# Late modulation rows summed on GpSimd from the channel stage on, and the scores of four memory steps kept for the other direction

## What is computed

```python
mod = silu(c) @ w_ada + b_ada                       # 6 * 1024 numbers: sh1, sc1, g1, sh2, sc2, g2
u = layernorm(x) * (1 + sc1) + sh1
proj = u @ w_in                                     # q, k, v, o, gates and the latents of attention
q, k = silu(conv5(proj[q, k]) + conv_b)             # along the tokens, a channel at a time
h = mlstm_scan(q, k, v, i_fw, f_fw) + flip(mlstm_scan(flip(q, k, v), i_bw, f_bw))
# one step of a scan, on a chunk of 128 tokens:
#   w   = exp(d_log - m_t)                          (128 x 128, masked to the past)
#   s   = (q k^T) * w
#   num = a * (q C) + s v ;  h = num / max(|den|, exp(-m_t))
#   C  <- decay * C + (k * wg)^T v
x = layernorm(alpha * x + (1 + g1) * mixer(u));  u = layernorm(x) * (1 + sc2) + sh2   # then the experts, with g2
```

## Time and profile before

| | us |
|---|---|
| median of 3 runs | 1534.51 (1533.08 to 1534.63) |
| the profiled execution | 1535.46, its span 1533.5 |
| TensorE busy | 1487.1 (97% of the span) |
| VectorE busy | 565.2 (37%) |
| ScalarE busy | 357.5 (23%) |
| GpSimd busy | 97.5 (6%) |

### The profile page before, as it was taken

The page is one execution under the profiler, slowest core; times in us unless marked ns, Lnnn a source line. Parts: engine busy times, 40 slices in busy tenths (PEclk is TensorE's granted clock), DMA queues, the critical chain, the costliest instruction groups (busy, mean ns, idle before and its releaser), DMA issues. The chain is left out here.

```text
span 1533.5 us, 19984 instructions
## 1 busy us (share of the span) xinstructions
PE 1487.1 (97%) x7403; PEld 818.7 (53%) x7404; DVE 565.2 (37%) x1134; ACT 357.5 (23%) x738; POOL 97.5 (6%) x97
## 2 busy tenths in 40 slices
PE   7999999999989999999999899999999999999997
PEld 4555554447868666674555554444444444444443
DVE  2222126567769433334867711111011011011118
ACT  1122122137624344352111010110111111111111
POOL 0000002000000000000000011111111111111110
PEclk9999999999999999999999899999999999999999
DMA  9401011128730200004111589869789879999965
GB/s 343 159 28 41 0 8 31 41 69 248 248 114 2 110 0 0 0 0 154 76 56 55 192 344 391 370 243 415 317 327 425 314 314 414 423 385 399 425 282 208
DMA packets 101798, 305.51 MB, mean 199 GB/s; under 512 B 18353, under 2 KB 61661, under 8 KB 92536
## 3 DMA queue, kind: packets, MB, share of 16 engines
q1 hardware_dynamic: 93064, 287.08, 48.6%
q0 software_dynamic: 8064, 16.80, 3.0%
q10 hardware_dynamic: 624, 1.03, 0.2%
HBM read 289.86 MB, written 25.76 MB: 206 GB/s over the span
## 5 line engine op out<-in xcount | busy, mean ns | idle before, releaser
L1908 PE MATMUL ps<-w_down_sb,hidT 128*128 x320 | 153.4, 612 | 0.0
L457 PE MATMUL ps<-w_in_tok,uT 128*128 128x512 f32 (+2 forms) x384 | 141.5, 529 | 0.0
L1892 PE MATMUL ps<-w_gate_sb,x_slotsT 128*128 x320 | 140.7, 593 | 0.7 <-ACT x_slotsT L1991 0.7
L1892 PE MATMUL ps<-w_up_sb,x_slotsT 128*128 x320 | 140.6, 592 | 0.0
L1563 PE MATMUL ps<-uT,hT 128*128 128x512 f32 x256 | 112.8, 594 | 0.0
L624 PE MATMUL ps<-uT,mod 128*128 128x512 f32 x256 | 111.0, 594 | 0.8 <-PEq L213 0.8
L2145 DVE TENSOR_TENSOR hid<-silu_g,ps 128x512 f32<-128x512 f32 x20 | 13.8, 688 | 258.0 <-PE ps L1892 258.0
L457 PEld LDWEIGHTS ps<-w_in_tok,uT 128*128 128x128 f32 x384 | 72.7, 190 | 65.3 <-issue 43.9
L1892 PEld LDWEIGHTS ps<-w_gate_sb,x_slotsT 128*128 128x128 f32 x320 | 60.8, 190 | 76.8 <-issue 76.8
L1892 PEld LDWEIGHTS ps<-w_up_sb,x_slotsT 128*128 128x128 f32 x320 | 60.9, 190 | 76.5 <-issue 76.5
L1908 PEld LDWEIGHTS ps<-w_down_sb,hidT 128*128 128x128 f32 x320 | 55.9, 189 | 65.1 <-issue 64.3
(11 more groups left out here) (405 smaller groups left out, 1926.7 us busy)
## 6 DMA issues: line engine op xcount, KB each, us to landing
light_gate_sb<-in_w_gate SPq DMA_DIRECT2D x20, 2048.0 KB
light_up_sb<-in_w_up SPq DMA_DIRECT2D x20, 2048.0 KB
light_down_sb<-in_w_down SPq DMA_DIRECT2D x20, 2048.0 KB
w_gate_sb<-in_w_gate SPq DMA_DIRECT2D x12, 2048.0 KB
w_up_sb<-in_w_up SPq DMA_DIRECT2D x12, 2048.0 KB
w_down_sb<-in_w_down SPq DMA_DIRECT2D x12, 2048.0 KB, 23.1
mod<-in_w_ada SPq DMA_DIRECT2D x8, 1024.0 KB, 8.1
w_ada_late<-in_w_ada SPq DMA_DIRECT2D x8, 1024.0 KB, 6.8
```

The lines of the kernel that those rows point to most:

```text
L457: mm = nc.tensor.matmul(ps[:, 2 + g, 0:n], self.uT[:, k, t * P:(t + 1) * P], wt[:, k, c0:c0 + n], start=k == 0, stop=k == KD - 1)
L1892: m = m_.matmul(ps[:, bank, :], xT[:, k, :], wt[:, bass.ds(buf, 1), k, :].rearrange("p a f -> p (a f)"), start=k == 0, stop=k == KD - 1)
L1908: m = m_.matmul(ps[:, 5 + half, :], hT[:, k, :], wd[:, bass.ds(buf, 1), k, half * 512:half * 512 + 512].rearrange("p a f -> p (a f)"), sta ...
```

## The change

- The sum over the eight slices of a piece moves from TensorE to GpSimd (`late_part`): it multiplies the tile by `ca` (spread over the 256 columns) in place, then adds 4 + 4, 2 + 2 and 1 + 1 slices. It leaves one row to a partition in `late_parts` (8 places). `spread` then sums over the partitions with a matrix of ones. `partial` and ScalarE's copy go.
- Pieces 0 to 7 are summed in the channel stage, pieces 8 to 15 in the memory stage, where piece n waits for `spread(n - 8)`. SP issues the loads of pieces 0 to 8 between the channel weights; those from piece 2 on wait until the tile that they overwrite has been summed. `LATE_HOME` says which of the two tiles a piece has; in the channel stage the second is `qkT[:, 6:8]`, so the silu of chunk 6 waits for piece 5.
- `scores` runs for steps 0 to 3 only. ScalarE copies each to `hdir` (`kept`), in the place of the other direction's rows of that chunk, and `weighted` of steps 4 to 7 reads it there.

```diff
...
+AHEAD = 8
+LATE_HOME = (0, 1, 0, 1, 0, 1, 0, 0, 0, 1, 0, 1, 0, 1, 0, 1)
...
+        self.w_late0 = pieces(self.mod[:, 0:2, :])
+        self.late_parts = self.sb("late_parts", [P, AHEAD, PC], ctx=up)
+        w_late = [self.w_late0, pieces(self.qkT[:, 6:8, :])]
...
+                def modulation(n, free):
+                    if free:
+                        sp.wait_ge(self.s_lpart, free)
+                    at = EARLY * 512 + n * PC
+                    sp.dma_start(w_late[LATE_HOME[n]], w_ada[:, :, at:at + PC]).then_inc(self.s_lw[LATE_HOME[n]], 16)
+                modulation(0, 0)
                 weights(2)
+                modulation(1, 0)
                 weights(3)
+                modulation(2, 1)
+                modulation(3, 2)
                 sp.wait_ge(s_atc, 2)
...
                 weights(4)
+                modulation(4, 3)
                 weights(5)
+                modulation(5, 4)
                 sp.wait_ge(s_M, 2)
...
                 weights(6)
+                modulation(6, 5)
                 weights(7)
+                modulation(7, 7)
...
-                sp.dma_start(self.w_late0, w_ada[:, :, EARLY * 512:EARLY * 512 + PC]).then_inc(self.s_lw[0], 16)
+                modulation(8, 8)
...
             @block.gpsimd
             def _(pool):
...
                 nc.gpsimd.tensor_tensor(self.hm[:], self.hm[:], mg.unsqueeze(1).to_broadcast([P, TT, H * HD]), ALU.mult).then_inc(s_gm, 1)
                 pool.wait_ge(s_gm, 1)
+                ch = Chain(pool, s_lsum)
+                for n in range(AHEAD):
+                    self.late_part(pool, ch, n, w_late[LATE_HOME[n]])
+                    pool.wait_ge(self.s_lpart, n + 1)
...
             @block.tensor
             def _(pe):
...
                     act.wait_ge(s_cv[j], c // 2 + 1)
+                    if c == 6:
+                        act.wait_ge(self.s_lpart, 6)
                     a.activation(self.qkT[:, c, :], acc[:, j, :], ACT.Silu).then_inc(s_act[j], 1)
...
+    def late_part(self, pool, ch, n, w):
+        g = self.nc.gpsimd
+        pool.wait_ge(self.s_lw[LATE_HOME[n]], 16 * LATE_HOME[:n + 1].count(LATE_HOME[n]))
+        ch.link(g.tensor_tensor(w, w, self.ca[:].unsqueeze(2).to_broadcast([P, KD, PC]), ALU.mult))
+        ch.link(g.tensor_tensor(w[:, 0:4, :], w[:, 0:4, :], w[:, 4:8, :], ALU.add))
+        ch.link(g.tensor_tensor(w[:, 0:2, :], w[:, 0:2, :], w[:, 2:4, :], ALU.add))
+        g.tensor_tensor(self.late_parts[:, n % AHEAD, :], w[:, 0, :], w[:, 1, :], ALU.add).then_inc(self.s_lpart, 1)
     def mlstm(self, up):
...
-            part = sb("late_partial", [P, PC])
...
             @block.sync
             def _(sp):
                 def modulation(n):
-                    if n > 1:
-                        sp.wait_ge(s_lp, n - 1)
+                    if n > AHEAD + 1:
+                        sp.wait_ge(s_lpart, n - 1)
...
-                    sp.dma_start(w_late[n % 2], w_ada[:, :, at:at + PC]).then_inc(s_lw[n % 2], 16)
+                    sp.dma_start(w_late[LATE_HOME[n]], w_ada[:, :, at:at + PC]).then_inc(s_lw[LATE_HOME[n]], 16)
...
                 def maxima(i, d):
...
                 maxima(*HALVES[2])
                 maxima(*HALVES[3])
                 bias(0)
-                modulation(1)
+                modulation(AHEAD + 1)
                 maxima(*HALVES[4])
                 maxima(*HALVES[5])
                 for k in range(len(HALVES) - 2):
-                    modulation(k + 2)
...
                         maxima(*HALVES[k + 6])
+                    if k % 2 == 0 and 2 <= k <= 12:
+                        modulation(AHEAD + 1 + k // 2)
...
                         bias(k // 4 + 1)
...
-                sp.wait_ge(s_lp, len(HALVES) - 1)
+                sp.wait_ge(s_lpart, len(HALVES) - 1)
...
+            @block.gpsimd
+            def _(pool):
+                ch = Chain(pool, s_lsum)
+                for n in range(AHEAD, len(HALVES)):
+                    pool.wait_ge(s_ls, n - AHEAD + 1)
+                    self.late_part(pool, ch, n, w_late[LATE_HOME[n]])
...
             @block.scalar
             def _(act):
...
+                def kept(i, d):
+                    if i >= TT // 2:
+                        return
+                    act.wait_ge(S["p"][d], i + 1)
+                    a.copy(self.hdir[:, 1 - d, chunk(i, d), :], ps[:, d, :]).then_inc(s_keep[d], 1)
...
+                kept(0, 0)
                 for k in range(len(HALVES)):
...
                         decays(*HALVES[k + 3])
-                    act.wait_ge(s_lp, k + 1)
-                    if k > 0:
-                        act.wait_ge(s_ls, k)
-                    a.copy(part[:], ps[:, 7, 0:PC]).then_inc(s_lpc, 1)
...
                         keys(*HALVES[k + 2])
+                    if k + 1 < len(HALVES):
+                        kept(*HALVES[k + 1])
...
             @block.tensor
             def _(pe):
...
                 def scores(i, d):
+                    if i >= TT // 2:
+                        return
                     if i > 0:
...
+                        pe.wait_ge(s_keep[d], i)
...
-                def partial(n):
-                    pe.wait_ge(s_lw[n % 2], 16 * (n // 2 + 1))
+                def spread(n):
+                    pe.wait_ge(s_lpart, n + 1)
...
-                    for k in range(KD):
-                        j = 32 * (k % 4)
-                        m = t.matmul(ps[j:j + 32, 7, 0:PC], self.ca[:, k:k + 1].to_broadcast([P, 32]), w_late[n % 2][:, k, :], start=k < 4, stop=k >= 4)
-                    m.then_inc(s_lp, 1)
-                def spread(n):
-                    pe.wait_ge(s_lpc, n + 1)
-                    t.matmul(ps[:, 7, PC:2 * PC], self.c(C_SUM), part[:], start=True, stop=True).then_inc(s_ls, 1)
+                    t.matmul(ps[:, 7, PC:2 * PC], self.c(C_ONE), self.late_parts[:, n % AHEAD, :], start=True, stop=True).then_inc(s_ls, 1)
...
                 scores(0, 0)
                 key_turns(0, 0)
                 scores(0, 1)
-                partial(0)
                 key_turns(0, 1)
...
                     outer(i, d)
-                    if k > 0:
-                        partial(k)
                     memory(i, d)
...
                         scores(*HALVES[k + 2])
...
                 def weighted(i, d):
-                    dve.wait_ge(S["sc"][d], i + 1)
+                    if i < TT // 2:
+                        dve.wait_ge(S["sc"][d], i + 1)
+                        kq = ps[:, d, :]
+                    else:
+                        dve.wait_ge(s_keep[1 - d], TT - i)
+                        kq = self.hdir[:, d, chunk(i, d), :]
...
                     if i > 0:
...
-                    v.scalar_tensor_tensor(out=p[:, d], in0=ps[:, d, :].rearrange("p (h t) -> p h t", h=H), scalar=QSCALE, in1=w[:, d],
+                    v.scalar_tensor_tensor(out=p[:, d], in0=kq.rearrange("p (h t) -> p h t", h=H), scalar=QSCALE, in1=w[:, d],
...
```

More of the change, by code:

```diff
@@ L528, in project_channels @@
         self.s_lw = [self.sem(f"w_ada_late_loaded{j}") for j in range(2)]
-        self.w_late0 = self.mod[:, 0:2, :].rearrange("p a (k n) -> p (a k) n", n=PC)
+        self.s_lpart = self.sem("late_part_summed")
+        s_lsum = self.sem("late_channel_sums")
+        pieces = lambda ap: ap.rearrange("p a (k n) -> p (a k) n", n=PC)
+        self.w_late0 = pieces(self.mod[:, 0:2, :])
+        self.late_parts = self.sb("late_parts", [P, AHEAD, PC], ctx=up)
+        w_late = [self.w_late0, pieces(self.qkT[:, 6:8, :])]
         w_ada = self.i["w_ada"].rearrange("(p k) n -> p k n", k=KD)
@@ L822, in mlstm @@
         s_v, s_c0 = self.sem("ml_dve"), self.sem("ml_state0")
+        s_keep = [self.sem(f"ml_scores_kept{d}") for d in range(2)]
         s_lw = self.s_lw
         s_lb = [self.sem(f"b_ada_late_loaded{r}") for r in range(4)]
-        s_lp, s_lpc, s_ls, s_late = (self.sem(n) for n in ("late_partial", "late_partial_copied", "late_spread", "late_ready"))
+        s_lsum, s_ls, s_late = (self.sem(n) for n in ("late_sums", "late_spread", "late_ready"))
+        s_lpart = self.s_lpart
         w_ada = self.i["w_ada"].rearrange("(p k) n -> p k n", k=KD)
```

## The result

The changed kernel takes **1579.37 us** (median of 4 runs, 1577.6 to 1582.11) against 1534.57 us (4 runs, 1533.08 to 1535.36): a ratio of 1.0295 with an interval of 1.0281 to 1.0309, slower. 1586 was forecast, in a range of 1521 to 1606. The profiled execution took 1577.74 us with a span of 1575.9 us, 42.4 us more than before.

A forecast was written before the change was run, and what follows sets the result against it. TensorE was taken as the bound, VectorE close behind. Span 1533.5 + 33 (channel stage) + 18 (memory stage) = 1584.5; with 1.96 outside the span 1586.5, so 1586 us against the median, range 1521 to 1606.

The forecast's parts named there:

- The hold: Both stages: VectorE operations with both inputs in SBUF wait until the running GpSimd operation ends, as L723 did.
- Rival one: Both stages: two-input operations are not held; +4 and -17.9, 1521 us, if no tap exceeds 1.4 us; chance 0.21.
- Rival two: Both stages: VectorE gets the exclusive port repeatedly, `a_by_head` nearly on time, GpSimd late; +24 and +5, 1564 us; chance 0.13.
- 29 us for `a_by_head`: Channel stage, before the third chunk: VectorE and GpSimd alternate, so TensorE resumes at 280.5 instead of 251.37.
- +2 for the clock: Channel stage: after 29 us idle TensorE's granted clock falls, costing 2 us.
- +2 for piece 7: Channel stage's end: piece 7 runs against the last convolution, exposing up to a 4.4 us operation; 2 us taken.
- 33: Channel stage in total: 29 + 2 + 2 us later, bounds +4 and +40.
- +18 for the memory stage: Memory stage: net 18 us longer with pieces 8 to 15 on GpSimd; bounds -17.9 and +32.
- 17.9: Memory stage without contention: 72.2 us against 90.1, so 17.9 us saved.
- beside other work: Memory stage, ScalarE: 16 copies go and 8 of 128x512 (0.59 us for one that size) come, beside other work.
- the path followed: Memory stage: half and piece in step at 9.7 us, eight pieces 78 us, seven halves left; 112 us, +22.
- the random case: Memory stage with waits at random instead: a half 7.8 us, ten done by 82.6, five left; +13.

The follow-up runs named there:

- the writes: Changed kernel with GpSimd's operations on each piece replaced by memsets of about the same time; no total compared, marks at 345.66 and 425.99, memory stage 80.3 us.
- the copies: Changed kernel with GpSimd's two-input operations on each piece replaced by one-input copies; no total compared, marks at 348.55 and 438.54 us.
- the last experiment: Against the kernel before: scores kept, first kept copies earlier, pieces 0 to 7 on GpSimd in tokens stage, 8 to 15 on TensorE; 1521.85 us, ratio 0.990.

## Why the prediction was right, and where its terms were off

**The hold: right.** The step chosen by inference, that VectorE operations with both inputs in SBUF are held to the end of the running GpSimd operation, is shown: by L756, L757, L760 and the taps, and by the writes and the copies, where only GpSimd's reading differs. Rival one (1521) falls: a tap was 2.6 us (10.43 / 4), and its mark was 1.4. Rival two falls: `a_by_head` was not on time.

**29 us for `a_by_head`: 17.8, mis-sized in the count, the durations and the overlap.** It was 31.5 us of GpSimd (14 operations) and 10.1 of VectorE, one after the other from 238.6 to 280.2. It went from 239.51 to 269.38. GpSimd did 12 operations, the last of them the end of piece 2; in the kernel with the sums alone, with the same code here, it did 13 and the wait was 21.8 us, so 17.8 is one of at least two outcomes. They are shorter than L610's rate gave: the product takes 3.60 us (1.76 ns an element, not 2.16), the adds about 2.35, 1.27 and 0.72 where nothing holds them (in the tokens stage of the last experiment). So 3 x 7.94 = 23.8 us, and with the wait for piece 2's load (2.50 us; a wait that I had excluded) 26.3. Of VectorE's 10.1 us only some 3.5 are left, GpSimd's gaps of 0.08 included: an operation of 0.43 us hardly lengthens what GpSimd does (piece 0 runs at 3.62, 2.41, 1.33 and 0.79), and a tap of 1.31 lengthens an add by 0.85.

**+2 for the clock: right.** The four chunks behind the gap take 57.25 us against 55.10, 2.15 more. The windows right behind the gap:

```profile
269.95:274.50 4.55, 4.55 (x7) 1.92 (x7) 4.51 (x2) 0.00 (x0) 4.47 (x2) 0.52 0.00 0
274.50:327.00 52.50, 52.50 (x123) 22.99 (x121) 39.50 (x23) 6.10 (x6) 29.11 (x11) 1.00 0.24 69
```

After 17.8 idle us TensorE runs 4.55 us at the lower level, 1.2 GHz (0.52), and then at 2.4 GHz.

**+2 for piece 7: 3.9.** The wait before the memory stage is 5.83 us against 1.97. I had counted the last convolution; the operations that were held are the small ones ahead of it (L819 to L823: 1.3 us before, 7.0 now, three of them held). A term was missing: weights late by 1.2 us (the 1.19 at 328.60). The third chunk starts 18.6 us later (the wait 17.8, a later start of the stage 0.6, 0.2 the rest); 18.6 + 2.15 + 1.2 + 3.9 and 0.3 elsewhere are 26.2, where I had 33.

**+18 for the memory stage: 17.4, with other parts.** The undisturbed stage is 80.3 us (writes) to 83.9, so 16 to 19.5 us saved, where 17.9 was worked out. Half and piece go in step in 8.8 us, not 9.7, by the same overlap. But piece 8 begins 9.6 us behind the first outer product (371.62 to 381.19) and not 4.6: it waits for the first spread, and that stands behind the 2.82 us for the first kept copy, which I had put at nothing ("beside other work"), and behind the lower clock that follows (0.80 on the mean from 371.62 to 380.04). GpSimd also waits 7.92, 1.44 and 0.67 us for loads. From piece 8's start to piece 15's end it is 82.7 us (78 forecast), 10.0 of them these waits, in which halves run nearly free (5.0 us from the outer product at 421.61 to the next at 426.60). By the forecast's own marks, the first outer product and the transposes behind the last half, the stage is 107.6 us (371.62 to 479.27; 90.1 before), 17.6 more; the path followed gave 112.2, and I had taken 4 us off for the random case. Against that path piece 8 starts 5.0 us later and the eight pieces take 4.7 more, but only four halves (15.4 us) are left behind piece 15 and not seven (29.6). The errors nearly cancel; the right total is partly luck.

**The kept scores.** In the 17.9 they stood for 7.1 us of TensorE; alone they bring 3.3 in the stage, and beside the sums they cost about 8 us in the stage and 4.6 in the total (1579.37 and 1574.81, not timed side by side, and the two channel stages differ by 3.1 us on the same code, so the difference is rough). Of the 8.2 us, 4.9 lie before piece 8's start, in the wait for the kept copy and the lower clock behind it. The piece work between is even 2.8 us shorter (82.7 against 85.5), with 10.0 us of load waits against 14.5, and what follows piece 15 is 6.2 longer (19.7 against 13.5). That `pT` is held is shown (up to 4.02 us). What stays open is how much of the rest is `pT` and how much the changed rhythm of loads: no run separates them.

**The sum.** 33 + 18 = 51 was forecast, 26.2 + 17.4 = 43.6 measured.

## What to carry to other kernels

Before work is given to an idle engine, ask what it shares with the engine that is next in line: eight pieces, 65 us of GpSimd, cost 1.5 us beside a stage where VectorE is busy a third of the time, and sixteen cost 44 us net beside stages where it is busy 60 to 70% without them. Here one row, a tiny operation held to the end of a large one on another engine, was enough to suspect the sign, though not to show it for operations with two inputs; the size came from counting how many of the large ones fit ahead of the one write that the bounding engine waits for. And a value moved from PSUM to SBUF to save work can bring its reader under the same hold, and the copy that moves it can itself be waited for.

## What was not expected of the hardware

- A held pair costs less than its sum: tap and add of 1024 elements 1.31 + 2.35 = 3.66 us of work in 3.28 (263.09 to 266.37), copy and tap 2.35 in 1.97, so about 0.38 us of each pair overlap.
- GpSimd's rate depends on the operation: 2.16 ns an element for L610's product, 1.76 for that of a piece (both have a repeated second operand, L610's read in stretches of 512 elements, the piece's one number 256 times in a row; no run shows whether that or the size of 4096 against 2048 makes the difference), 2.3 for the add of 1024 and 2.8 for that of 256, about 1.0 for a copy and 0.88 for a memset of 2048. Chained operations follow each other in 0.06 to 0.08 us.
- GpSimd's memsets hold copies and TENSOR_SCALARs of VectorE (a TENSOR_SCALAR of 8 elements took 1.83 us beside one, 0.17 without; the copy above 0.69 instead of 0.22), but not the two-input taps, `qs`, masks or small products.
